# Attention queries: one plain load and four two-head transposes per tile, low parts written to the other half of the partitions

## What is computed

```python
qg = q.reshape(B, Tq, KV, R, HD)
logits = jnp.einsum('bqgrd,bqkgd->bqgrk', qg, k_sel).astype(jnp.float32) * (HD ** -0.5)
...
p = jax.nn.softmax(logits, axis=-1)
out = jnp.einsum('bqgrk,bqkgd->bqgrd', p.astype(v.dtype), v_sel)
```

## Time and profile before

| what | value |
|---|---|
| median of 3 runs | 1501.06 us (1497.01 to 1502.92) |
| the profiled execution | 1498.33 us, span 1496.5 us |
| mean granted PE clock | 0.988 |
| PE busy | 1434.4 us, 96% of the span |
| DVE, ACT, POOL busy | 67%, 50%, 54% |
| chain that ended last | PE 62%, DVE 4%, POOL 3%, issue 2%, ACT 2% |
| the attention stage | from about 485 to 641 us of the span |

### The profile page before, as it was taken

The page is one execution under the profiler, slowest core; times in us unless marked ns, Lnnn a source line. Parts: engine busy times, 40 slices in busy tenths (PEclk is TensorE's granted clock), DMA queues, the critical chain, the costliest instruction groups (busy, mean ns, idle before and its releaser), DMA issues.

```text
span 1496.5 us, 23333 instructions
## 1 busy us (share of the span) xinstructions
PE 1434.4 (96%) x7796; PEld 1182.6 (79%) x7796; DVE 1005.3 (67%) x1900; ACT 753.0 (50%) x1550; POOL 806.9 (54%) x685
## 2 busy tenths in 40 slices
PE   6998899999999899999999999999999999999995
PEld 6986687878777678878878888888887888888874
DVE  5368577777886665523568656666669777777787
ACT  5467477777577788723353433433353333233232
POOL 3310456666652343012465645654668977877888
PEclk9999899999999999999999999999999999999998
DMA  7310312111107452134323343343365444444344
GB/s 232 84 27 21 102 38 67 43 48 52 53 25 170 110 154 49 43 113 137 124 71 111 138 165 111 141 162 124 141 237 185 166 154 152 141 142 164 99 159 168
DMA packets 123886, 172.99 MB, mean 116 GB/s; under 512 B 46424, under 2 KB 95992, under 8 KB 121592
## 3 DMA queue, kind: packets, MB, share of 16 engines
q1 hardware_dynamic: 119840, 140.02, 30.2%
q10 hardware_dynamic: 3928, 31.48, 5.1%
HBM read 119.59 MB, written 51.88 MB: 115 GB/s over the span
## 4 chain that ended last, share of the span: by engine, by line
PE 62%; DVE 4%; POOL 3%; issue 2%; ACT 2%; POOLq 0%; DVEq 0%; ACTq 0%
PE wide L389 10%; PE wide L390 10%; PE wide L391 10%; PE paired L389 8%; PE paired L390 8%; PE paired L391 8%; PE paired L2008 2%; PE wide L1979 2%; PE paired L1990 2%; POOL acc L3076 1%; POOL acc L3085 1%; DVE qT L1857 0%; DVE ob_mT_lo L2392 0%; PE paired L2304 0%; PE paired L1965 0%
## 5 line engine op out<-in xcount | busy, mean ns | idle before, releaser
L2201 POOL TENSOR_TENSOR wu_lo<-raw_u,wu_hi 128x512 fp32r<-128x512 f32 x64 | 97.0, 1528 | 148.0 <-ACT wu_hi L2196 147.9
L389 PE MATMUL paired<-w_hi,aT_hi 128*128 128x512 f32 x320 | 132.1, 413 | 1.4 <-PEq L424 1.4
L391 PE MATMUL paired<-w_hi,aT_lo 128*128 128x512 f32 x320 | 126.4, 395 | 0.0
L390 PE MATMUL paired<-w_lo,aT_hi 128*128 128x512 f32 x320 | 126.0, 394 | 0.0
L374 POOL TENSOR_TENSOR w_lo<-stage,w_hi 128x512 fp32r<-128x512 f32 (+1 forms) x50 | 64.4, 1304 | 99.5 <-ACT w_hi L369 99.5
L3115 DVE TENSOR_TENSOR acc<-wide,acc 128x512 f32<-128x512 f32 x116 | 79.4, 687 | 45.4 <-PE wide L391 45.2
L1070 ACT ACTIVATE spare<-scores,sl_key 128x768 bf16<-128x768 f32 (+2 forms) x96 | 100.1, 1042 | 10.5 <-DVE sl_key L1176 3.8
L2201 POOL TENSOR_TENSOR wu_lo<-w_sum,wu_hi 128x512 fp32r<-128x512 f32 x60 | 96.5, 1640 | 0.0
L389 PE MATMUL paired<-aT_hi,wu_hi 128*128 128x512 f32 x240 | 95.0, 396 | 1.5 <-DVE acc L3115 1.2
L390 PE MATMUL paired<-aT_lo,wu_hi 128*128 128x512 f32 x240 | 93.6, 390 | 0.0
L391 PE MATMUL paired<-aT_hi,wu_lo 128*128 128x512 f32 x240 | 93.5, 390 | 0.0
(11 more groups left out here) (399 smaller groups left out, 4681.8 us busy)
## 6 DMA issues: line engine op xcount, KB each, us to landing
f_scratch<-f_out ACTq DMA_DIRECT2D x15, 1984.0 KB, 6.1
w_all<-f_scratch SPq DMA_DIRECT2D x32, 896.0 KB, 4.8
raw_u<-in_w_up SPq DMA_DIRECT2D x16, 1024.0 KB, 5.3
raw_d<-in_w_down SPq DMA_DIRECT2D x16, 1024.0 KB, 6.8
stage<-in_w_in SPq DMA_DIRECT2D x32, 256.0 KB, 3.3
stage<-mix_scratch SPq DMA_DIRECT2D x9, 512.0 KB, 4.1
h_scratch<-ob_h SPq DMA_DIRECT2D x9, 512.0 KB, 2.9
fn_h<-h_scratch SPq DMA_DIRECT2D x9, 512.0 KB, 7.8
```

The source lines that it names most:

```text
L389: nc.tensor.matmul(out, lhs[0], rhs[0], start=first, stop=False, skip_group_check=onto)
L390: nc.tensor.matmul(out, lhs[0], rhs[1], start=False, stop=False, skip_group_check=onto)
L391: return nc.tensor.matmul(out, lhs[1], rhs[0], start=False, stop=last, skip_group_check=onto)
L2201: self.nc.gpsimd.tensor_tensor(self.room.wu[1][:, s], self.source(i), self.room.wu[0][:, s].bitcast(F32), ALU.subtract).then_inc(self.lo_d ...
```

## The change

A query set's eight heads are loaded once, as a plain copy of 128 rows of 2 KB, into one of four buffers (`qrow` keeps its size). Four transposes instead of eight turn two heads at a time: the heads of key group 0 land on partitions 0 to 63, those of group 1 on 64 to 127. This is one piece and one bank. ACT then makes two copies of 64x512, each to its own half, and counts `q_hi` once, behind the second. DVE makes two subtractions of 64x512, each reading one half and writing the low part to the other half of the same head's place, and counts `q_lo` once. For group 1 the high part is now on partitions 64 to 127 and the low part below. The keys' piece stays as it was; a set has two pieces instead of three, and all counts and the rotation of banks follow.

```diff
--- before.py
+++ after.py
@@ -1530,7 +1530,7 @@
     kp, mn = sb("kp", [P, 2, 2, P]), sb("mn", [P, 2, HEADS])
     den, rden = sb("den", [P, HEADS]), sb("rden", [P, HEADS])
     vp = sb("vp", [P, 2, 2, P])
-    qrow = sb("qrow", [P, 2, HEADS, 2, HD])
+    qrow = sb("qrow", [P, 4, HEADS * HD])
     pr = sb("probs", [P, 3, D])
     psT = sb("psT", [P, 2, 3, P])
     os_ = sb("os", [P, 2, HD])
@@ -1596,7 +1596,7 @@
         return [n + 1] if rest == 0 and n + 1 < TILES else []
 
 
-    pieces_of = lambda n: [0] if n == 0 else [3 * n - 2, 3 * n - 1, 3 * n]
+    pieces_of = lambda n: [0] if n == 0 else [2 * n - 1, 2 * n]
     uses = []
     for u in range(END):
         for n in queries_at(u):
@@ -1612,14 +1612,15 @@
     position = {x: i for i, x in enumerate(uses)}
     bank_of = lambda kind, n: tp[position[kind, n] % 3]
 
-    def turned_views(n, p, part, bank):
-
-        i = pieces_of(n).index(p)
-        if i == 2:
-            t = Q_ORDER[n]
-            return kT[part][:, :, t * P:(t + 1) * P], bank[:, 0:2 * P].rearrange("p (g i) -> p g i", g=KV)
-        rows_of = slice(0, P) if part == 0 else slice(HD, P)
-        return (qT[rows_of, n % 2, 4 * i:4 * i + 4], bank[rows_of].rearrange("p (h i) -> p h i", h=4))
+    def key_views(n, part, bank):
+        t = Q_ORDER[n]
+        return kT[part][:, :, t * P:(t + 1) * P], bank[:, 0:2 * P].rearrange("p (g i) -> p g i", g=KV)
+
+    def query_views(n, g, bank):
+
+        own, other = slice(g * HD, g * HD + HD), slice(HD - g * HD, P - g * HD)
+        cells = qT[:, n % 2].rearrange("p (m g) i -> p m g i", g=KV)[:, :, g]
+        return cells[own], cells[other], bank[own].rearrange("p (m i) -> p m i", m=4)
 
     skew = lambda off, dims: bass.AP(toep_d.tensor, off, dims)
     head_size = NEW * (TOEP + 1)
@@ -1630,12 +1631,11 @@
             sp.wait_ge(q_turned, pieces_of(n - 2)[-1] + 1)
         sp.wait_ge(aq_out[n % 4], 16 * (n // 4 + 1))
         t = Q_ORDER[n]
-        q = aq_d[t * P:(t + 1) * P].rearrange("p (h d) -> p h d", d=HD)
         if n == 0:
             sp.dma_start(srow[:], aq_d[t * P:(t + 1) * P]).then_inc(q_in[0], 16)
             return
         k = ck_pf[t * P:(t + 1) * P].rearrange("p (h d) -> p h d", d=HD)
-        sp.dma_start(qrow[:, n % 2], repeated(q, 2, 2)).then_inc(q_in[n % 2], 16)
+        sp.dma_start(qrow[:, n % 4], aq_d[t * P:(t + 1) * P]).then_inc(q_in[n % 2], 16)
         sp.dma_start(krow[:, n % 2], repeated(k, 2, 2)).then_inc(q_in[n % 2], 16)
 
     def caches_in(sp, s):
@@ -1710,7 +1710,13 @@
                     continue
                 if n >= 3:
                     act.wait_ge(qk_done, HEADS * (n - 2))
-                nc.scalar.activation(*turned_views(n, p, 0, bank), ACT.Copy).then_inc(q_hi, 1)
+                if p == pieces_of(n)[1]:
+                    nc.scalar.activation(*key_views(n, 0, bank), ACT.Copy).then_inc(q_hi, 1)
+                    continue
+                for g in range(KV):
+                    high, _, src = query_views(n, g, bank)
+                    mm = nc.scalar.activation(high, src, ACT.Copy)
+                mm.then_inc(q_hi, 1)
 
         def keep_keys(s):
             act.wait_ge(k_turned, s + 1)
@@ -1850,11 +1856,16 @@
                 dve.wait_ge(q_hi, p + 1)
                 if n == 0:
                     continue
-                out, src = turned_views(n, p, 1, bank_of("query", p)[:])
-                high = turned_views(n, p, 0, bank_of("query", p)[:])[0]
-                if pieces_of(n).index(p) < 2:
-                    high = out
-                nc.vector.tensor_tensor(out, src, high.bitcast(F32), ALU.subtract).then_inc(q_lo, 1)
+                bank = bank_of("query", p)[:]
+                if p == pieces_of(n)[1]:
+                    out, src = key_views(n, 1, bank)
+                    high = key_views(n, 0, bank)[0]
+                    nc.vector.tensor_tensor(out, src, high.bitcast(F32), ALU.subtract).then_inc(q_lo, 1)
+                    continue
+                for g in range(KV):
+                    high, low, src = query_views(n, g, bank)
+                    tt = nc.vector.tensor_tensor(low, src, high.bitcast(F32), ALU.subtract)
+                tt.then_inc(q_lo, 1)
 
         for u in range(END):
             for n in queries_at(u):
@@ -1920,8 +1931,8 @@
                 bank = claim("query", p)
                 if n == 0:
                     blocks = [srow[:, m * P:(m + 1) * P] for m in range(4)]
-                elif i < 2:
-                    blocks = [qrow[:, n % 2, 4 * i + h].rearrange("p b d -> p (b d)") for h in range(4)]
+                elif i == 0:
+                    blocks = [qrow[:, n % 4, m * P:(m + 1) * P] for m in range(4)]
                 else:
                     blocks = [krow[:, n % 2, g].rearrange("p b d -> p (b d)") for g in range(KV)]
                 for k, block in enumerate(blocks):
@@ -1971,7 +1982,7 @@
             if u >= 2:
                 pe.wait_ge(lg_done, u - 1)
             L = P * (t + 1)
-            pe.wait_ge(q_lo, 3 * (t + 1))
+            pe.wait_ge(q_lo, 2 * (t + 1))
             g, m = h // 4, h % 4
             for c0 in range(0, L, 512):
                 w = min(512, L - c0)
```

## The result

The changed kernel takes 1513.74 us (median of 4 runs, 1511.14 to 1515.18) where the kernel before, run beside it, takes 1500.12 us: a ratio of 1.0086, with a 95% interval of 1.0071 to 1.0101. A second measurement in another session gave 1.0078 (1.0064 to 1.0092). It is **slower by 13 us**, outside the forecast range, which ended at 1511. The loss lies in the attention stage: from PE's first transpose of a query set to the last start of a turning of probabilities it lasts 166.7 us (488.03 to 654.7) instead of 152.3 (485.67 to 638.0).

What follows compares the result with a forecast made beforehand. PE was taken to stand in the attention stage for the queries' low parts, on a path through PE, ACT and DVE. Set delays summed to 4.2 us, added to the 1501.06 us median: 1505.3 us, range 1498 to 1511.

Steps and rivals of the forecast that it cites:

- The bound and the place: Attention stage: PE waits for the queries' low parts written at L1857, four stops at L1990, one of 1.9 us at L1979.
- The path: PE's transposes, ACT's copies, DVE's subtractions, then PE again: later by 0.27 to 0.74 us a set, 4.2 us over eight.
- the forecast of the next logits: Set 8: the last three turns wait for the low part, so the next logits start at 607.29, not 606.55: +0.74 us.
- PE's start: Set 1: PE waits for the keys' part, behind the queries' on DVE, and starts 0.53 us later, at 489.41.
- PE's saved transposes: Eight sets lose four each, 3.7 us of PE time, spent standing at the next bank; rival that it stays saved: 0.14.
- Copies as long as before: ACT's 64x512 copy taken equal to 128x512; at half, 4.4 us would cancel the sum.
- no second pass: A DVE subtraction reading one half and writing the other taken to cost nothing extra, against up to 0.69 us.
- Loads at nothing: Query load halved to 256 KB, in 2 KB pieces, four buffers: hidden, so costed at nothing; without cover some 2.8 us a set.
- the clock: Low stretch of three one-microsecond slices after set 1's pause: could lengthen, shift or drop, 1.5 us either way; taken as nothing.
- the second pass: Rival: writing to the other half costs DVE 16 x 0.69 = 11.0 us more on the path, 1516.3 us; chance 0.10.
- the delay of DVE's and ACT's own later work: DVE's own logits move back about half a microsecond; PE needs them two steps later, so costed at nothing.

Runs made afterwards that it cites:

- fills: Changed kernel with transposes of the identity of no use added on PE ahead of its q_lo wait; with 28 at set 1, 12 at later sets: 1505.4 us.
- Keys first: Changed kernel with a set's keys turned ahead of its queries: 1507.39 us (1.0049) with the joint signal, 1500.29 us (0.9996) with a signal per copy.

## Why the prediction was wrong

**The bound and the place: right.** The stops of PE for L1857's low parts were the place to look, and they grew, from 4.5 to 13.7 us.

**The path: right, a little small.** The sum gave 4.2 us. Without the added low clock the changed kernel is 3.5 to 5.7 us slower. At set 8 the forecast of the next logits, 3.73 us after the set's start, met 3.68. The two copies take 1.18 to 1.20 us, not 1.09: at 592 ns each they do not overlap, where two of 596 did. The subtractions take 1.39, not 1.41. At set 1 PE's start came later than forecast by ACT's late start, which no term of the sum had. PE's saved transposes bought nothing in the changed kernel, as the forecast said: they were spent standing.

**Copies as long as before, and no second pass: right.** 592 against 596 ns, 688 against 690 ns. (The Trainium skill, page Vector Engine (DVE) Microarchitecture Reference, section The reshape front-end and per-opcode configuration, allows for that; the trace now shows it.) That each subtraction starts only when the last has ended is seen in 1.39 us for two of 0.69, where the two within a half took 1.30; the rule of page VectorE: DVE Perf Modes of the Trainium skill holds here.

**Loads at nothing: right** within two or three microseconds, by the run with the doubled load.

**The step that failed is the clock.** The prediction bounded it by 1.5 us either way and took nothing, because it looked at the one low stretch that the trace of before shows, behind set 1's stop, and asked only what becomes of that one. But the stop at set 1 is one of eight. In the short tiles at the stage's start PE is not fully busy even with fills (17.43 of 20 us), and about a microsecond more of standing at each set, half of it the longer path and half the saved transposes, was enough for the granted clock to fall again and again up to 540 us and once more after 560: 27.4 us at the lower level instead of 3.4. That costs 6 to 8 us, more than everything that was computed, and carried the time past the end of the range. The rival that ended near the measured time, the second pass, was not what happened.

What stays open is how much of the direct 3.5 to 5.7 us is PE's stop at the banks and how much the delay of DVE's and ACT's own later work, which the sum put at nothing. Keys first shows that the order of the banks decides 4 to 5 us, but stops and low stretches shrink together there. Nor is the joint signal's price the same everywhere: with keys first, taking it away gains 8 us while the low clock above that of the kernel before falls only from 8.8 to 5.2 us (counted as in the table), so there most of the price is not the clock's.

## What to carry to other kernels

A joint signal behind two copies looks like less synchronisation and breaks a pipeline of three engines: signal each piece when it is done, and let the piece that is needed last be the one that is waited for last. Where PE is not fully busy, cost a longer stop twice, once for itself and once for the clock that it may let fall; the granted clock by window shows where that threatens, and work of no use in the gap is a cheap test of it.

## What the runs showed of the hardware that was not expected

The kernel sped up when PE was given more to do: 28 + 7 x 12 = 112 added transposes, some 13 us of PE work at 0.116 us each, made the changed kernel 0.55 to 0.63% faster. A change of half a microsecond in one wait per set, with the same work on PE, took the time at 1.2 GHz in the stage from 3.4 to 17 us in the profiled executions (5.6 us more on the average of all executions). (The Trainium skill, page TensorE: Matmul & The Clock Gate, Part 1, says that the throttled level is the default and that activity releases it; these runs agree.)
